# First attention layer of a two-block network: TensorE takes the next step's scores at the end of a step instead of at its start

## The chip, the cores and the metric

The kernel runs on one core of one Trainium2 chip. The metric is the device time of one execution in microseconds, as the median over several executions. A lower number is better. In the text TensorE is PE (its weight loads PEld), VectorE is DVE, ScalarE is ACT, GpSimd is POOL and SyncE is SP, as in the profile.

## What is computed

512 tokens of width 1024 go through two blocks. The first block is a recurrent and convolutional mixer and a layer that gathers expert rows for each token. The second has two attention layers, each followed by a SwiGLU layer. The change lies in the first of these attention layers only. For each head it adds three attentions over the same queries:

```python
s = einsum('bsgrd,bngd->bgrsn', q, k_cmp) * scale        # 31 compressed keys
p, denom, _ = masked_softmax(s + bias_c, dist_c >= 0)
o_cmp = einsum('bgrsn,bngd->bsgrd', p / maximum(denom, 1e-30), v_cmp)
...
o_sel = ...   # selected blocks of 64 keys; with 8 of 8 blocks all causal keys
o_win, _ = banded_attention(q, kwn, vwn, WIN - 1, 1, rel_bias)   # 256 keys back
o = g[..., 0:1] * o_cmp + g[..., 1:2] * o_sel + g[..., 2:3] * o_win
return o.reshape(B, S, D_MODEL) @ w_out
```

There are 16 heads of 64 channels and 4 groups of keys and values.

## The kernel before, in words

The program is written engine by engine, and each engine's queue is in the order of the Python code. Semaphores order the engines among each other. Nothing is scheduled automatically. The first attention layer's loop has 32 steps (STEPS = 8 * TT): eight pairs of heads, and for each pair four blocks of 128 queries (qt = s mod 4). A step handles the two heads of its pair, "half" 0 and 1, which sit on partitions 0 to 63 and 64 to 127. For each half there are three branches: "sel" with 128 (qt + 1) keys, "win" with at most 384, and "cmp" with 31. For one step, these are the pieces of work:

- `scores(s)` on PE (L1542): six products into four banks of the accumulator memory. "sel" has a bank of its own for each half, "win" and "cmp" share one. There is one set of banks, so a product waits until DVE has read that bank's scores of the step before (`bank_read`).
- `row_max(s)` on DVE (L1614): six instructions, each adding the bias table to the scores, writing the sum to `pA` and taking the row's extreme. It waits for `scores_ready`; its first instruction needs the first product, its second needs the fifth (`SCORES_BEFORE`).
- `exponentials(s)` on ACT (L1669), with the row sums.
- `inverse(s)` (L1632, L1634) and `scale(s)` (L1641, L1645) on DVE: the inverse of the row sums times the gates, then the scaling of all three branches of half 0 and the "sel" branch of half 1. POOL scales "win" and "cmp" of half 1 (L1704).
- `turn(s)` on PE (L1556): 6, 10, 14 or 16 transposes of the scaled weights, in chunks of four, into three banks in turn. A chunk with only half 0 needs `scaled`; one with half 1 needs POOL's `scaled_rest` too. A chunk also waits until the chunk three before has been copied out.
- `copies(s)` on ACT (L1592) and, for a step's last chunk, `last_copy(s)` on DVE (L1592 for full blocks, L1595 for the "cmp" blocks) into `ptA`.
- `values(s)` on PE (L1572): products of the transposed weights with the values, added up in one bank for both halves. It waits for all of the step's chunks in `ptA`.

The steps overlap. In iteration s, DVE does row_max(s), last_copy(s-2), inverse(s-1), scale(s-1); ACT does exponentials(s), copies(s-1). [...] SP loads the bias tables for a later pair of heads, released by `bank_read`.

Of the kernel before, what the change touches and what calls it, by code (L numbers as in the profile page):

```python
# [163 lines left out]
def program(nc, t):  # L164

    with ExitStack() as ctx:
# [1294 lines left out]
        STEPS = 8 * TT  # L1461
# [16 lines left out]
        def branches(s, half):  # L1478

            it, qt = divmod(s, TT)  # L1480
            gp = it // GR
            g, lo = 2 * gp + half, 64 * half
            rows, keys, cols = slice(lo, lo + 64), P * (qt + 1), slice(P * qt, P * qt + P)
            kv = slice(64 * g, 64 * g + 64)
            k0 = max(0, qt - 2)
            wide = keys - P * k0
            q, base = proj[rows, it, cols], 928 * half
            return {
                "sel": Branch(half, 2 * half, 0, keys, base, q, proj[rows, 12 + gp, 0:keys],
                              tabA[:, it % 2, half, 512 - keys:512], 1, [vtok[:, 0, x, kv] for x in range(qt + 1)]),  # L1490
                "win": Branch(half, 2 * half + 1, 0, wide, base + 512, q, proj[rows, 16 + gp, P * k0:keys],
                              tabA[:, it % 2, half, 896 - wide:896], 2, [vtok[:, 1, x, kv] for x in range(k0, qt + 1)]),
                "cmp": Branch(half, 2 * half + 1, 384, NCMP, base + 896, q, kcmp[rows, gp, :],
                              tcmp[:, heads(it)[half], 24 - 8 * qt:24 - 8 * qt + NCMP], 0, [vcmp[0:NCMP, kv]])}
# [6 lines left out]
        def turn_list(s):  # L1501

            sides = [branches(s, half) for half in range(2)]
            full = [(half, b) for half in range(2) for x in ("sel", "win") for b in sides[half][x].blocks]
            return full + [(half, sides[half]["cmp"].blocks[0]) for half in range(2)], len(full)

        def turn_chunks(s):

            order, full = turn_list(s)
            whole = full // 4 * 4  # L1510
            return [order[x:x + 4] for x in range(0, whole, 4)] + [order[whole:]]

        def chunk_no(s):

            return sum(len(turn_chunks(x)) for x in range(s))
# [5 lines left out]
        def chunk_copied(eng, s, c):  # L1521

            if c == len(turn_chunks(s)) - 1:
                eng.wait_ge(LA.last_copied, s + 1)
            else:
                eng.wait_ge(LA.pt_copied, act_chunks(s) + c + 1)
# [4 lines left out]
        def turn_bank(no):  # L1531
            return TURN_BANKS[no % len(TURN_BANKS)]

        def nsa_pe(pe, compressed_values):
            bank_of = {}

            def scores(s):
                for x, (name, half) in enumerate(PE_ORDER):
                    b = branches(s, half)[name]
                    if s:  # L1540
                        pe.wait_ge(LA.bank_read, PER * (s - 1) + READS_BEFORE[x])
                    pe.matmul(b.scores, b.q, b.keys, start=True, stop=True).then_inc(LA.scores_ready, 1)  # L1542

            def turn(s):
                for c, chunk in enumerate(turn_chunks(s)):
                    no = chunk_no(s) + c
                    turns = len(TURN_BANKS)
                    if no - turns in bank_of:
                        chunk_copied(pe, *bank_of[no - turns])
                    bank_of[no] = s, c  # L1550
                    other = max(half for half, _ in chunk)
                    pe.wait_ge(LA.scaled, 2 * s + 1 + other)
                    if other:
                        pe.wait_ge(LA.scaled_rest, s + 1)
                    for x, (_, (at, width, _)) in enumerate(chunk):
                        tr = pe.transpose(ps[0:width, turn_bank(no), P * x:P * x + P], pA[:, s % 3, at:at + width], ident)  # L1556
                    tr.then_inc(LA.turned, 1)

            def values(s):
                it, qt = divmod(s, TT)  # L1560
                for c in range(len(turn_chunks(s))):
                    chunk_copied(pe, s, c)
                if s == 0:
                    pe.wait_ge(cmp_copied, 2)
                if qt == 0 and it:
                    pe.wait_ge(LA.o_drained, it)
                order, _ = turn_list(s)
                sides = [[(x, b) for x, (half, b) in enumerate(order) if half == side] for side in range(2)]
                for y in range(len(sides[0])):
                    for half in range(2):  # L1570
                        x, (_, width, v) = sides[half][y]
                        mm = pe.matmul(ps[64 * half:64 * half + 64, OUT_BANK, P * qt:P * qt + P], v,  # L1572
                                       ptA[0:width, s % 2, P * x:P * x + P], start=y == 0, stop=y == len(sides[0]) - 1)
                mm.then_inc(LA.pv_done, 1)

            scores(0)
            compressed_values()
            for s in range(STEPS + 2):
                if s + 1 < STEPS:
                    scores(s + 1)  # L1580
                if s >= 2:
                    values(s - 2)
                if 1 <= s <= STEPS:
                    turn(s - 1)

        def copy_chunk(copy, s, c, done):

            chunk = turn_chunks(s)[c]
            full = sum(width == P for _, (_, width, _) in chunk)
            src, dst = bank(turn_bank(chunk_no(s) + c)), ptA[:, s % 2, 512 * c:512 * c + P * len(chunk)]  # L1590
            if full:
                ins = copy(dst[:, 0:P * full], src[:, 0:P * full])  # L1592
            if full < len(chunk):
                w = chunk[-1][1][1]
                ins = copy(dst[0:w, P * full:P * len(chunk)], src[0:w, P * full:P * len(chunk)])  # L1595
            ins.then_inc(done, 1)
# [426 lines left out]
        def layer_a_pe(pe):  # L2023
# [57 lines left out]
            pe.wait_ge(vt_copied, 4)  # L2081
            pe.wait_ge(cmp_copied, 1)
            nsa_pe(pe, compressed_values)
            pe.wait_ge(LA.o_drained, 8)
            out_project(pe, "a_out", "a_o")
# [985 lines left out]
```

## Time and profile before

| | before |
|---|---|
| median of 3 runs | 2892.04 us (2891.43 to 2892.5) |
| profiled execution | 2893.09 us, span 2891.0 us |
| PE busy | 2705.6 us (94%) |
| DVE busy | 1883.0 us (65%) |
| POOL busy | 1185.4 us (41%) |
| ACT busy | 843.4 us (29%) |
| the loop of the change, 1603.40 to 1757.90 | 154.50 us; PE 146.78, PEld 112.79, DVE 130.69, ACT 130.00, POOL 53.10 busy |

The profile comes from one profiled execution. The span is the time between the first and the last instruction; the rest of the execution's time lies around it. A busy share is an average over all stages, and the loop in question is 5% of the span. PE's matmuls overlap in the array, so their busy time is not time at its peak. "Granted clock" is TensorE's clock as a share of 2.4 GHz.

### The profile page before, as it was taken

How to read it: one execution, taken by the hardware profiler on the slowest of the kernel's cores; microseconds unless marked ns; L12 is line 12 of the kernel's file. 1: busy time of each engine (PE TensorE's matmuls, PEld its weight loads, DVE VectorE, ACT ScalarE, POOL GpSimd, SP SyncE). 2: the span in 40 equal slices, each digit the busy share in tenths (PEclk: the TensorE clock that was granted, in tenths of full speed). 3: DMA queues.
4: the chain of work that ended last, by engine and by line, in shares of the span. 5: the costliest groups of instructions: out<-in, count | busy, mean ns of one | idle time of the engine just before them, and what ended most of it. 6: DMA issues, size and time to landing. Idle time of an engine off the chain costs nothing.

```text
span 2891.0 us, 35803 instructions
## 1 busy us (share of the span) xinstructions
PE 2705.6 (94%) x12080; PEld 1729.4 (60%) x12080; DVE 1883.0 (65%) x4890; ACT 843.4 (29%) x1653; POOL 1185.4 (41%) x837
## 2 busy tenths in 40 slices
PE   8999999999877777799999999999999999999999
PEld 3364454444333332344447777888888877788887
DVE  8997888888888888778766786444223336554411
ACT  4731211111111111121123785222132127522222
POOL 5314444444444444444440233444444434444443
PEclk9999999999999999999999999999999999999999
DMA  4169999999999999999996121222323222222322
GB/s 132 61 236 371 418 414 418 421 421 420 417 421 419 420 421 414 419 418 420 420 420 239 59 69 59 95 94 94 107 89 100 90 67 67 66 95 96 103 101 79
DMA packets 130308, 700.38 MB, mean 242 GB/s; under 512 B 16694, under 2 KB 28886, under 8 KB 64343
## 3 DMA queue, kind: packets, MB, share of 16 engines
q0 software_dynamic: 74352, 543.04, 45.6%
q1 hardware_dynamic: 54760, 153.30, 16.0%
q10 hardware_dynamic: 1072, 2.41, 0.2%
q8 instruction: 75, 1.23, 0.2%
q14 instruction: 49, 0.40, 0.0%
HBM read 696.41 MB, written 2.28 MB: 242 GB/s over the span
## 4 chain that ended last, share of the span: by engine, by line
PE 49%; DMA 18%; issue 14%; DVE 8%; POOL 7%; ACT 3%; POOLq 0%; DVEq 0%; SPq 0%; ACTq 0%
DMA arena<-in_peer_uv,arena 18%; PE ps L543 16%; PE ps L883 15%; POOL w_lo L420 6%; PE ps L2379 3%; DVE arena L1216 2%; PE ps L911 2%; ACT arena L1669 1%; PE ps L2031 1%; PE ps L795 1%; DVE arena L1227 1%; PE ps L1572 1%; PE ps L1556 1%; PE ps L773 1%; PE ps L1542 1%
## 5 line engine op out<-in xcount | busy, mean ns | idle before, releaser
L883 PE MATMUL ps<-arena 128*128 128x512 f32 x2048 | 955.9, 611 | 143.4 <-DVE arena L1227 142.9
L1350 POOL DMA_INDIRECT arena<-in_peer_uv,arena x512 | 570.2, 1114 | 783.2 <-PE ps L883 719.7
L883 PEld LDWEIGHTS ps<-arena 128*128 128x128 f32 x2048 | 383.6, 194 | 651.4 <-issue 384.5
L1216 DVE CUSTOM_DVE_ANT_0 arena<-arena,sq 128x1024 f32<-128x1024 f32 x512 | 607.3, 1224 | 192.5 <-DMA arena<-in_peer_uv,arena 189.5
L420 POOL TENSOR_TENSOR w_lo<-ring,w_hi 128x1024 fp32r<-128x1024 f32 (+1 forms) x156 | 407.3, 2611 | 514.9 <-ACT w_hi L433 514.9
L543 PE MATMUL ps<-n_hi,w_hi 128*128 128x512 f32 x992 | 388.0, 391 | 0.5 <-issue 0.3
L543 PE MATMUL ps<-n_hi,w_lo 128*128 128x512 f32 x992 | 386.5, 390 | 0.0
L543 PE MATMUL ps<-n_lo,w_hi 128*128 128x512 f32 x992 | 382.4, 390 | 0.2 <-DVE n_lo L470 0.2
L1043 ACT ACTIVATE dots_gel<-dots_gel,tok_scale 128x2 f32<-128x2 f32 x256 | 75.7, 296 | 1000.0 <-DVE dots_gel L1216 999.7
L433 ACT CAST w_hi<-ring 128x1024 fp32r<-128x1024 f32 (+1 forms) x156 | 174.6, 1119 | 644.4 <-PE ps L543 644.4
L543 PEld LDWEIGHTS ps<-n_hi,w_hi 128*128 128x128 f32 x992 | 186.3, 188 | 40.5 <-issue 2.4
L543 PEld LDWEIGHTS ps<-n_lo,w_hi 128*128 128x128 f32 x992 | 186.3, 188 | 40.0 <-DVE n_lo L470 0.8
L543 PEld LDWEIGHTS ps<-n_hi,w_lo 128*128 128x128 f32 x992 | 186.3, 188 | 38.7
L1227 DVE TENSOR_SCALAR arena<-consts,dots_gel,tcmp 128x128 f32<-128x128 f32 x512 | 161.6, 368 | 30.5 <-ACT dots_gel L1043 15.5
L599 DVE TENSOR_TENSOR h<-ps,h 128x512 f32<-128x512 f32 x32 | 22.1, 691 | 218.9 <-PE ps L543 218.9
L1425 DVE TENSOR_TENSOR arena<-ps,rstd 128x512 f32<-128x512 f32 x44 | 30.4, 692 | 200.4 <-PE ps L543 200.4
L543 PE MATMUL ps<-hid_hi,w_hi 128*128 128x512 f32 x352 | 137.3, 390 | 1.3 <-POOL w_lo L420 1.3
L543 PE MATMUL ps<-hid_lo,w_hi 128*128 128x512 f32 x352 | 137.1, 390 | 0.0
L543 PE MATMUL ps<-hid_hi,w_lo 128*128 128x512 f32 x352 | 137.1, 390 | 0.0
L1704 POOL TENSOR_SCALAR arena<-arena 128x384 f32<-128x384 f32 (+2 forms) x64 | 53.1, 839 | 167.7 <-DVE arena L1634 167.7
L2379 PE MATMUL ps<-n,ring 128*128 128x512 f32 x256 | 114.0, 603 | 8.0 <-DMA ring<-in_w_in 7.8
L911 PE MATMUL ps<-n,ring 128*128 128x384 f32 x320 | 111.9, 487 | 0.0
(364 smaller groups left out, 3614.4 us busy)
## 6 DMA issues: line engine op xcount, KB each, us to landing
ring<-in_a_up SPq DMA_DIRECT2D x44, 512.0 KB, 3.5
ring<-in_b_up SPq DMA_DIRECT2D x44, 512.0 KB, 3.5
ring<-in_a_in SPq DMA_DIRECT2D x40, 512.0 KB, 7.8
ring<-in_b_q SPq DMA_DIRECT2D x24, 512.0 KB, 3.5
ring<-in_a_down SPq DMA_DIRECT2D x16, 704.0 KB, 4.1
ring<-in_b_down SPq DMA_DIRECT2D x16, 704.0 KB, 4.0
ring<-in_w_in SPq DMA_DIRECT2D x16, 512.0 KB, 3.5
arena<-in_peer_uv,arena POOLq DMA_INDIRECT x512, 10.8
```

The lines of the kernel that those rows point to most:

```text
L420: pool.tensor_tensor(w_lo[:, j % 2, 0:kt * P], ring[:, j, 0:kt * P], w_hi[:, j % 2, 0:kt * P], ALU.subtract).then_inc(split_lo, 1)
L433: act.copy(w_hi[:, j % 2, 0:kt * P], ring[:, j, 0:kt * P]).then_inc(split_hi, 1)
L543: mm = pe.matmul(bank(j // 2 if two else j), w[:, j % 2, cols], r[:, x, :], start=no == 0 and not (two and j % 2), stop=no == len(passes) ...
L883: mm = pe.matmul(bank(2 * (tt % 2) + q), diag[:, no % DIAGS, r, :], uvrow[p][r][:, D + 512 * q:D + 512 * q + 512], start=slot + r == 0, st ...
L911: mm = pe.matmul(ps[:, p % 2, 0:EARLY], ring[:, p % RING, k * P:(k + 1) * P], n[:, k, 0:EARLY], start=k == 0, stop=k == DK - 1)
L1043: act.activation(gel[:, p, :], dots[:, p, :], ACT.Gelu_apprx_tanh, scale=tok_scale[:, tt:tt + 1]).then_inc(gel_ready, 1)
L1216: ins = dve.tensor_tensor_reduce(out=u, in0=u, in1=ntok[:, tt, :], scale=1.0, scalar=0.0, op0=ALU.mult, op1=ALU.add, accum_out=dots[:, p, ...
L1227: ins = dve.tensor_scalar(diag[:, no % DIAGS, r, :], ident, gel[:, p, r:r + 1], gate_now[:, slot + r:slot + r + 1], ALU.mult, ALU.mult)
L1350: pool.indirect_dma_start(uvrow[p][r], None, t["peer_uv"], bass.IndirectOffsetOnAxis(ap=expert_id[:, tt, slot + r:slot + r + 1], axis=0)). ...
L1425: dve.tensor_tensor(gated[:, pr, :], bank(2 * pr + 1), rstd[:, :], ALU.mult).then_inc(tile_drained, 1)
L1704: ins = pool.tensor_scalar(pr, pr, invA[:, s % 3, 1, b.slot:b.slot + 1], None, ALU.mult)
L2379: mm = pe.matmul(bank(u % RING), ring[:, u % RING, k * P:(k + 1) * P], ns[k], start=k == 0, stop=k == DK - 1)
```

## The change

In `nsa_pe`, the iteration s of PE's loop issued scores(s+1), values(s-2), turn(s-1). Now it issues values(s-2), turn(s-1), scores(s+1). Nothing else is edited.

```diff
             for s in range(STEPS + 2):
-                if s + 1 < STEPS:
-                    scores(s + 1)
                 if s >= 2:
                     values(s - 2)
                 if 1 <= s <= STEPS:
                     turn(s - 1)
+                if s + 1 < STEPS:
+                    scores(s + 1)
```

The queue of PE in the middle of the loop, around the scores with 256 keys (L1542 scores, L1572 values, L1556 transposes), before:

```order
L1572 MATMUL ps<-arena 64x128 x10
L1556 MATMUL ps<-consts,arena 128x128 x12
L1556 MATMUL ps<-consts,arena 31x128 x2
L1542 MATMUL ps<-arena 128x256 x4
L1542 MATMUL ps<-arena 128x31 x2
L1572 MATMUL ps<-arena 64x128 x14
L1556 MATMUL ps<-consts,arena 128x128 x14
L1556 MATMUL ps<-consts,arena 31x128 x2
L1542 MATMUL ps<-arena 128x384 x4
```

The same place with the change:

```order
L1572 MATMUL ps<-arena 64x128 x14
L1556 MATMUL ps<-consts,arena 128x128 x14
L1556 MATMUL ps<-consts,arena 31x128 x2
L1542 MATMUL ps<-arena 128x256 x4
L1542 MATMUL ps<-arena 128x31 x2
L1572 MATMUL ps<-arena 64x128 x16
L1556 MATMUL ps<-consts,arena 128x128 x4
L1556 MATMUL ps<-consts,arena 31x128 x2
L1542 MATMUL ps<-arena 128x384 x4
```

The scores with 256 keys stood ahead of 14 products with the values and 16 transposes, and now stand behind them. The cyclic order scores, values, transposes is the same; what changes is which step's scores stand between a step's transposes and the next values: those of one step earlier.

The start of the loop, as the difference of PE's queue with its waits left out:

```order
 L1542 MATMUL ps<-arena 128x256 x4
 L1542 MATMUL ps<-arena 128x31 x2
+L1556 MATMUL ps<-consts,arena 128x128 x4
+L1556 MATMUL ps<-consts,arena 31x128 x2
 L1542 MATMUL ps<-arena 128x384 x4
 L1542 MATMUL ps<-arena 128x31 x2
-L1556 MATMUL ps<-consts,arena 128x128 x4
+L1572 MATMUL ps<-arena 64x128 x6
```

The scores of steps 0 and 1 keep their place; from step 2 on (128x384) a step's scores come behind the transposes of the step two before. The queues of DVE, ACT, POOL and SP are the same in both kernels.

## Rows read from the trace of the kernel before

**Rows 1.** Busy time by stretch: one round of four steps of the loop

```profile
core 0: us, PE busy (x) PEld busy (x) DVE busy (x) ACT busy (x) POOL busy (x), PEclk, DMA share, GB/s
1655.39:1673.95 18.56, 18.04 (x187) 13.89 (x188) 16.27 (x84) 15.97 (x59) 6.64 (x9) 1.00 0.17 57
```

**Rows 2.** Waits in the whole loop, 1603.4 to 1758 us

```profile
engine line waited for: us in total, times, longest us
...
DVE arena L1595 <- PE ps L1556: 10.8, 15, 2.1
...
DVE arena L1592 <- PE ps L1556: 7.1, 8, 2.0
...
PEld ps L1542 <- DVE arena L1614: 4.1, 18, 0.7
```

**Rows 3.** Timeline of one round, TensorE: start, duration, instruction, [idle before]

```profile
start us, us, engine line op out<-in xcount [idle before <-releaser]
...
1657.42 1.27 PE L1542 MATMUL ps<-arena 64*128 64x256 f32 x12
...
1660.46 2.04 PE L1556 MATMUL ps<-consts,arena 128*128 128x128 f32 x16
...
1662.44 1.70 PE L1542 MATMUL ps<-arena 64*128 64x384 f32 x12
...
1664.07 2.12 PE L1572 MATMUL ps<-arena 128*64 128x128 f32 x32
...
1666.12 0.87 PE L1556 MATMUL ps<-consts,arena 128*128 128x128 f32 x6
...
1666.93 1.92 PE L1542 MATMUL ps<-arena 64*128 64x512 f32 x12
```

**Rows 4.** Timeline of the same round, VectorE and GpSimd

```profile
1657.53 0.41 DVE L1595 COPY arena<-ps 31x256 f32<-31x256 f32 x1 [1.01 <-PE ps L1556]
...
1658.34 2.08 POOL L1704 TENSOR_SCALAR arena<-arena 128x384 f32<-128x384 f32 x2 [2.69 <-DVE arena L1634]
...
1660.49 0.42 DVE L1614 CUSTOM_DVE_ANT_0 arena<-ps,arena 128x256 f32<-128x256 f32 x1
...
1661.74 0.08 DVE L1614 DVE_READ_ACCUMULATOR2_ANT arena<- 128x1 f32 x1
...
1662.55 0.43 DVE L1592 COPY arena<-ps 128x256 f32<-128x256 f32 x1 [0.72 <-PE ps L1556]
...
1662.89 0.40 DVE L1595 COPY arena<-ps 31x256 f32<-31x256 f32 x1
...
1665.02 0.55 DVE L1614 CUSTOM_DVE_ANT_0 arena<-ps,arena 128x384 f32<-128x384 f32 x1
...
1666.67 0.08 DVE L1614 DVE_READ_ACCUMULATOR2_ANT arena<- 128x1 f32 x1
...
1667.84 1.49 POOL L1704 TENSOR_SCALAR arena<-arena 128x256 f32<-128x256 f32 x2 [3.03 <-DVE arena L1634]
...
1669.68 0.55 DVE L1614 CUSTOM_DVE_ANT_0 arena<-ps,arena 128x384 f32<-128x384 f32 x1
...
1671.46 0.41 DVE L1595 COPY arena<-ps 31x256 f32<-31x256 f32 x1
...
1672.26 1.94 POOL L1704 TENSOR_SCALAR arena<-arena 128x384 f32<-128x384 f32 x2 [2.93 <-DVE arena L1634]
```

**Rows 5.** Timeline, second iteration: GpSimd's scaling and the transposes it releases

```profile
1608.76 1.12 POOL L1704 TENSOR_SCALAR arena<-arena 128x128 f32<-128x128 f32 x2 [76.38 <-DVE arena L1634]
...
1609.99 0.61 PEld L1556 LDWEIGHTS ps<-consts,arena 128*128 128x128 f32 x6 [0.75 <-DVE arena L1645]
```

**Rows 6.** Timeline of the first two steps, where VectorE waits for scores

```profile
1603.43 0.86 PE L1542 MATMUL ps<-arena 64*128 64x128 f32 x12
...
1604.32 0.29 DVE L1614 CUSTOM_DVE_ANT_0 arena<-ps,arena 128x128 f32<-128x128 f32 x1
...
1605.18 0.08 DVE L1614 DVE_READ_ACCUMULATOR2_ANT arena<- 128x1 f32 x1
...
1605.41 1.52 PEld L1542 LDWEIGHTS ps<-arena 64*128 64x128 f32 x14
...
1606.72 0.42 DVE L1614 CUSTOM_DVE_ANT_0 arena<-ps,arena 128x256 f32<-128x256 f32 x1
```

**Rows 7.** Busy time by stretch: 1000 us of the expert stage

```profile
300.00:1300.00 1000.00, 869.53 (x2226) 392.25 (x2225) 834.43 (x2436) 162.33 (x341) 436.19 (x398) 0.98 1.01 419
```

## The prediction

> **What bounds the stage now.** I read the views in this order: busy time by stretch, the waits of the stage, then the timeline of one round of four steps. The edited loop is the compressed/selected/window attention of the first attention layer: 32 steps, in rounds of four that repeat. Step s has 1 to 4 key blocks (s mod 4 = 0 to 3); I call these widths 1 to 4. One round takes 18.56 us, and TensorE shows 18.04 us of it busy, VectorE 16.27, ScalarE 15.97, at a granted clock of 1.00 [rows 1]. So three engines are nearly full at once, which works only because each has something of another step to do while it waits. Over the whole loop VectorE idles 10.8 + 7.1 us for the transposes of a step's last chunk, and TensorE idles 4.1 us for VectorE's reading of the scores [rows 2]. Those are the only waits that this order of TensorE's work could be charged with; together 22 us.
>
> TensorE's busy time taken by itself would say that TensorE is the bound, and that its own order of work is then worth nothing: no change. The Trainium skill, Perfetto Trace Analysis, section Identifying the Most-Contended Engine, says that matmul busy time is no good measure and that the weight loads' share is better. By that reading there is slack here, since the loads are busy 13.89 of 18.56 us [rows 1]; the argument below needs only the order of dependences.
>
> In the timeline of the round [rows 3, 4], TensorE does scores, values, transposes, and again scores. VectorE reduces the scores of step s+1 while TensorE does values and transposes of older steps; at 1660.49 a reduction is under way and at 1660.46 the transposes start. The scores it reads (block at 1657.42) had been made 2.7 us before. That distance is the cover that the change takes away.
>
> **The change.** Nothing is added or removed: TensorE issues the same instructions, there is no DMA among them, and the other engines' queues are unchanged. 30 blocks of scores (steps 2 to 31) move from ahead of values(s-2) and turn(s-1) to behind them. turn(s-1) waits for scale(s-1) of VectorE and for the part that GpSimd scales. So the scores of s+1 now wait, through the queue, for scale(s-1); and VectorE's next work after scale(s-1) is the row reductions of s+1. Before, VectorE went from scale(s-1) into the reductions without a stop. Now it stands still while TensorE finishes the transposes and makes the scores. Values and transposes cannot slip earlier to pay for it, because values(s-2) need VectorE's last copy of s-2, which it issues behind the reductions of step s.
>
> The new cycle per step has three terms: VectorE's last copy, T from the end of that copy to the end of the transposes, and U from there to the end of the next row reductions.
>
> *Last copy.* 0.41 us where only two small blocks are copied (three of four steps), and 1662.55 to 1662.89 plus 0.40 = 0.74 us where there are two copies [rows 4]. Sum of a round 3 x 0.41 + 0.74 = 1.97 us. Its former waits of 1.01 and 0.72 us in these rows go, because the transposes are long done by then; that gain is inside this sum.
>
> *T.* GpSimd starts its scaling 0.40 us after the last copy ends (1657.53 + 0.41, then 1658.34) and takes 2.08, 1.49 and 1.94 us for the transposed steps of width 4, 2 and 3 [rows 4]. The first four transposes need only VectorE's half and come before it ends; the others wait for GpSimd. 16 transposes take 1660.46 to 1662.44 = 1.98 us and six 1666.12 to 1666.93 = 0.81 us [rows 3], so about 0.11 us each and 0.2 us to the next block. From GpSimd's last write to TensorE's next weight load is 0.11 us (1608.76 + 1.12, then 1609.99) [rows 5]. Hence, with the transposes behind the first four:
> width 4: 0.40 + 2.08 + 0.11 + 12 x 0.11 + 0.2 = 4.11;
> width 2: 0.40 + 1.49 + 0.11 + 6 x 0.11 + 0.2 = 2.86;
> width 3: 0.40 + 1.94 + 0.11 + 10 x 0.11 + 0.2 = 3.75.
> For width 1 the longer way is through the values of a width 4 step, 1664.07 to 1666.12 = 2.05 us [rows 3], so 0.11 + 2.05 + 0.81 = 2.97. Sum 13.69 us.
>
> *U.* The second reduction of a step needs five of the six score products, since window and compressed scores share a bank. The trace has two cases where VectorE stands waiting, as it will now always: the first two steps [rows 6]. At width 1 the second reduction starts 1604.32 - 1603.43 = 0.89 us after the block of scores, whose own busy time is 0.86; at width 2 it starts 1606.72 - 1605.41 = 1.31 us after, beside a block of 1.27 in the round [rows 3]. So it is the block plus 0.04. Blocks of width 3 and 4 take 1.70 and 1.92 us [rows 3], which gives 1.74 and 1.96. From the second reduction to the last: 1604.32 to 1605.18 = 0.86 [rows 6], 1660.49 to 1661.74 = 1.25, 1665.02 to 1666.67 = 1.65, 1669.68 to 1671.46 = 1.78 [rows 4]. U is 1.75, 2.56, 3.39, 3.74; sum 11.44 us.
>
> **Sum.** 1.97 + 13.69 + 11.44 = 27.10 us a round in place of 18.56 [rows 1]: +8.54, or 2.13 us a step. Times 30 moved blocks: **+64 us**. ScalarE's exponentials and copies (15.97 us busy per round) and GpSimd (6.64) fit in 27.1 us and stay off this cycle. Nothing later hides it: the products behind the loop need the last head's output. The profiled execution took 2893.1 us, 2.1 outside its span; it lies 1.1 above the median 2892.04. 2892 + 64 = **2956 us**.
>
> Bounds. Low: U supposes that a wide block must be nearly finished before the second reduction. If at every width it started after 0.89 us, as at width 1 [rows 6], a round would save 0.42 + 0.85 + 1.07 = 2.34, over 7.5 rounds 18 us: 2938. I take the block's length because width 2 follows it. High: each step gains two hand-overs that I price at 0.11 and 0.04. Were each 0.3 longer, a little above the mean idle of weight loads on VectorE in the loop (4.1 us over 18 times is 0.23) [rows 2], 30 x 0.6 = 18 us come on top: 2974.
>
> **Rivals.**
> - *TensorE's clock falls.* Its 18.04 busy us a round [rows 1] will stand in 27.1 us, 67% instead of 97%. In the expert stage, where TensorE shows 869.53 of 1000 us busy with waits between, the granted clock averages 0.98 [rows 7]: short falls from 2.4 to 1.2 GHz. At that rate it costs a few us here. If it stayed at 1.2 GHz throughout, the parts of TensorE on the cycle (transposes 1.52 + 0.81 + 0.86 + 1.30, values 2.05, scores 0.86 + 1.27 + 1.70 + 1.92 = 12.3 us a round) would double: +92 more, 3048. Against it: the idle gap of a step is at most 3.74 - 1.92 + 0.41 + 0.11 = 2.3 us (width 4), and rows 1 show 1.00 with many transposes. Full drop 4%, a partial one (above 2980) 6%.
>  The Trainium skill, TensorE: Matmul & The Clock Gate, Part 4: PE-mode transpose, says transposes do not count as busy work for the clock gate. By that rule the fall is likelier than I make it, with the same 3048 at the worst; the trace before, at 1.00 with transposes a third of TensorE's work, does not bear it out, though scores and values stood beside them.
> - *Faster.* If the reduced scores were not needed as soon as I say, the 10.8 + 7.1 + 4.1 us of rows 2 would vanish and nothing come in: 2870. It decides where transposes and scores end before VectorE is through with scale(s-1). The transposes wait for that very scaling, so this needs the dependence to be other than written: 2%.
> - *No change.* TensorE is really the bound and keeps its 18.04 us a round back to back, the order being immaterial: 2892. Busy shares speak for it, the chain through scale(s-1) against it: 3%.
> - *Half of it.* Faster VectorE and ScalarE instructions without contention, or a T where most transposes end before GpSimd does. Taking 0.7 us off each step's 2.13 leaves 43 us (2935), taking 1.4 leaves 22 (2914): about 2925, 5%. For it: the durations of rows 3 and 4 come from a loop with all engines busy. Against it: no row there shows one of these dependences skipped.
>
> **Numbers.** The forecast (2938 to 2974) has 80%, and the rivals have 10, 2, 3 and 5%. The range is 2930 to 2982: it holds the forecast's bounds, the upper end of the half case and a mild loss of clock. What a measurement can tell from no change is about 0.2% (6 us): faster 2%, within 0.2% 3%, slower 95%.
>
> **What would show it.** The loop should last about 64 us longer. A round should take near 27 us. VectorE's row reductions (L1614) should wait on L1542 in nearly all of 30 steps, some 2 to 3 us each; its waits of L1595 and L1592 on L1556, 17.9 us, should be nearly gone. TensorE's weight loads should wait for L1595, and its transposes for L1641, L1645 or L1704. The mean duration of instructions should stay. The prediction is wrong if L1614 does not wait, if a round stays under 24 us, or if the granted clock in the loop is well below 1.00.

## The result and the profile after

The changed kernel takes 2998.78 us (median of 4 runs, 2992.16 to 2999.77) against 2891.73 before: ratio 1.0369, 95% interval 1.0357 to 1.0381. It is 107 us slower. Forecast were 64 us and 2956, with 2982 as the upper end; the direction was right, the size was not.

The page of the changed kernel, busy times and the slices of TensorE, VectorE and clock:

```profile
span 2997.6 us, 35803 instructions
...
PE 2747.9 (92%) x12080; PEld 1758.6 (59%) x12080; DVE 1885.0 (63%) x4890; ACT 850.7 (28%) x1653; POOL 1183.5 (39%) x837
...
PEclk9999999999999999999998787999999999999999
```

The number of instructions is the same. The one new thing is the dip of the clock line in the slices of the loop: 8, 7, 8, 7. Everything that was lost was lost there. From the first scores to the first product behind the loop it was 1603.43 to 1758.66, 155.2 us; it is 1602.04 to 1865.57, 263.5 us. That is 108.3 us more, and what comes before and after differs by under 2 us.

The loop as one stretch of the changed kernel:

```profile
core 0: us, PE busy (x) PEld busy (x) DVE busy (x) ACT busy (x) POOL busy (x), PEclk, DMA share, GB/s
1602.50:1866.00 263.50, 190.68 (x1503) 144.17 (x1500) 134.25 (x648) 137.84 (x470) 53.17 (x64) 0.80 0.10 30
```

TensorE shows 190.68 us of it busy (72%) where it had 97% of a round [rows 1]. For the same instructions that is yet more busy time than the 146.78 us of before, and the granted clock averages 0.80. To read the counts: in these traces a matrix product leaves two records of TensorE and a transpose one. So x28 of L1572 is 14 products, and x16 of L1556 is 16 transposes.

Waits of the changed kernel, 1603 to 1880 us (engine, line, whom for, total, times, longest):

```profile
DVE arena L1614 <- PE ps L1542: 115.8, 45, 4.8
...
ACT arena L1669 <- DVE arena L1614: 64.7, 30, 4.2
...
PE ps L1572 <- DVE arena L1595: 45.9, 24, 2.4
...
DVE arena L1595 <- PE ps L1556: 3.9, 1, 3.9
...
DVE arena L1592 <- PE ps L1556: 1.9, 1, 1.9
```

The row reductions (L1614) wait 115.8 us for the scores. In the kernel before, 1603.4 to 1758 us, that wait came twice, and not in the steady loop:

```profile
DVE arena L1614 <- PE ps L1542: 8.6, 2, 7.9
```

The old waits for the transposes, 10.8 and 7.1 us [rows 2], are down to one each at the loop's end. TensorE in turn waits for VectorE's last copy ahead of the values. Each of the two stands while the other works.

The most useful view is busy time by stretch, with a stretch for each step, from the end of one step's row reductions to the end of the next. The number behind PEld, DVE, ACT and POOL is the granted clock. Widths 4, 1, 2, 3, 4, 1, 2 of the changed kernel:

```profile
1745.30:1752.31 7.01, 4.16 (x34) 2.76 (x34) 4.52 (x21) 4.32 (x15) 1.49 (x2) 1.00 0.00 0
1752.31:1758.21 5.90, 4.02 (x46) 3.24 (x46) 3.65 (x21) 4.22 (x15) 1.95 (x2) 1.00 0.52 156
1758.21:1765.25 7.04, 5.13 (x56) 4.26 (x56) 4.33 (x23) 4.10 (x18) 2.08 (x2) 1.00 0.02 3
1765.25:1773.88 8.63, 6.06 (x50) 4.76 (x50) 4.23 (x24) 4.02 (x15) 1.13 (x2) 0.80 0.00 0
1773.88:1782.53 8.65, 5.78 (x34) 3.81 (x34) 4.53 (x23) 4.42 (x15) 1.49 (x2) 0.80 0.01 2
1782.53:1791.00 8.47, 7.02 (x46) 5.86 (x46) 3.65 (x23) 4.42 (x15) 1.95 (x2) 0.60 0.88 261
1791.00:1798.03 7.03, 5.13 (x56) 4.26 (x56) 4.31 (x21) 4.09 (x18) 2.08 (x2) 1.00 0.29 117
```

At a clock of 1.00, widths 4, 1 and 2 take 7.01, 5.90 and 7.04 us. The prediction's terms give 7.01, 5.91 and 7.08. Widths 4 and 1 take 8.65 and 8.47 us where the clock was 0.80 and 0.60. So this one trace already separates the two parts of the loss, the new dependence and the clock, for three of the four widths. Of the 30 moved steps only nine ran at 1.00 throughout: the seven of width 2 and the one each of width 4 and width 1 shown here. No step of width 3 did.

The single instructions show both. Timeline of TensorE and VectorE in the changed kernel (start, duration):

```profile
1690.07 3.25 PE L1556 MATMUL ps<-consts,arena 128*128 128x128 f32 x14
...
1697.96 2.02 PE L1556 MATMUL ps<-consts,arena 128*128 128x128 f32 x16
...
1699.91 1.27 PE L1542 MATMUL ps<-arena 64*128 64x256 f32 x12
1700.64 0.43 DVE L1614 CUSTOM_DVE_ANT_0 arena<-ps,arena 128x256 f32<-128x256 f32 x1 [2.51 <-PE ps L1542]
...
1701.21 0.42 DVE L1614 CUSTOM_DVE_ANT_0 arena<-ps,arena 128x256 f32<-128x256 f32 x1
...
1707.65 3.20 PE L1542 MATMUL ps<-arena 64*128 64x384 f32 x12
```

VectorE stood 2.51 us for the block of scores that begins at 1699.91, and its second reduction starts 1.30 us after the block's start (1.31 was taken, from [rows 6]). 14 transposes took 3.25 us in a slow stretch, 16 took 2.02 in a fast one; the scores of width 3 took 3.20 us instead of 1.70 [rows 3].

### The profile page after: what moved, and what is told of

Its sections match the earlier page's. It is cut to its first block, busy times and chain, and to the rows that moved or that the text cites. A ratio compares the mean times of both kernels' runs of the same rounds, so it can differ in the third digit from the quotient of the medians.

```text
span 2997.6 us, 35803 instructions
## 1 busy us (share of the span) xinstructions
PE 2747.9 (92%) x12080; PEld 1758.6 (59%) x12080; DVE 1885.0 (63%) x4890; ACT 850.7 (28%) x1653; POOL 1183.5 (39%) x837
## 4 chain that ended last, share of the span: by engine, by line
PE 51%; DMA 18%; issue 14%; DVE 10%; POOL 6%; ACT 1%; POOLq 0%; DVEq 0%; SPq 0%; ACTq 0%
DMA arena<-in_peer_uv,arena 17%; PE ps L543 16%; PE ps L883 14%; POOL w_lo L420 6%; PE ps L2379 3%; DVE arena L1216 2%; PE ps L1556 2%; PE ps L911 2%; PE ps L1542 2%; PE ps L1572 2%; DVE arena L1614 1%; PE ps L2031 1%; DVE arena L1227 1%; PE ps L795 1%; PE ps L773 1%
## 5 line engine op out<-in xcount | busy, mean ns | idle before, releaser
L1614 DVE CUSTOM_DVE_ANT_0 arena<-ps,arena 128x384 f32<-128x384 f32 (+3 forms) x128 | 58.1, 473 | 125.7 <-PE ps L1542 123.8
L1572 PE MATMUL ps<-arena 128*64 128x128 f32 (+1 forms) x736 | 66.6, 330 | 63.5 <-DVE arena L1595 45.9
```

The costliest lines, as they stand in the source:

```text
L1614: dve.tensor_tensor_reduce(out=pA[:, s % 3, b.at:b.at + b.width], in0=b.scores, in1=b.tab, scale=1.0, scalar=-FLOOR, op0=ALU.add, op1=ALU.min,
```

## The experiments

Theory A: of the 107 us, 64 are the dependence at full clock, and 43 are TensorE working at 1.2 GHz in about 0.4 of the loop. Theory B: the 43 us are other new waits, and the clock is a side effect of no weight. All runs are compared with the kernel before on the same chip.

**Filler products.** They give TensorE more to do where it idles.

```diff
+            def fill(s, ns):
+                it, qt = divmod(s, TT)
+                if qt == 0 and it:
+                    pe.wait_ge(LA.o_drained, it)
+                for _ in range(ns[(s + 2) % TT]):
+                    pe.matmul(ps[:, OUT_BANK, P * qt:P * qt + P], ident, ident, start=True, stop=True)
...
                 if s + 1 < STEPS:
                     scores(s + 1)
+                    if s >= 2:
+                        fill(s - 1, (5, 8, 8, 8))
```

> The changed order, plus products that nobody reads (identity times identity, 128 columns, into the part of the values' bank that the next values overwrite), issued behind each block of scores from step 3 on: 5 behind a width 1 block, 8 behind the others, 211 in all. They lie where TensorE idles for VectorE's reductions and last copy. Theory A (of the 107 us, 64 are the new dependence at full clock and 43 are TensorE's clock falling to 1.2 GHz in 0.4 of the loop): the granted clock in the loop returns to 0.97 or more, and the time falls to 2950 to 2970 although TensorE has more to do. Theory B (the 43 us are longer waits that have nothing to do with the clock, and the clock figure is a side effect): no gain, 2995 to 3015, since the added products lengthen TensorE's queue.

Measured: 2958.77 us (2956.71 to 2960.94), ratio to before 1.0233 (1.0216 to 1.0250). With 211 more products the kernel is 40 us faster than the changed one. Busy time by stretch, one round, widths 4, 1, 2, 3:

```profile
1697.99:1705.00 7.01, 6.26 (x53) 4.72 (x51) 4.52 (x21) 4.31 (x15) 1.49 (x2) 1.00 0.01 4
1705.00:1710.90 5.90, 5.07 (x56) 4.20 (x55) 3.65 (x23) 4.23 (x15) 1.94 (x2) 1.00 0.51 157
1710.90:1717.93 7.03, 6.83 (x72) 5.85 (x72) 4.32 (x21) 4.09 (x18) 2.08 (x2) 1.00 0.01 2
1717.93:1725.06 7.13, 6.94 (x72) 5.68 (x71) 4.22 (x22) 4.02 (x15) 1.13 (x2) 1.00 0.00 0
sum 27.07, PE 25.10 PEld 20.45 DVE 16.71 ACT 16.65 POOL 6.65; mean PE 6.28 PEld 5.11 DVE 4.18 ACT 4.16 POOL 1.66
```

A round takes 27.07 us; 27.10 was predicted. Theory B falls: with the clock at 1.00 the widths 4, 1 and 2 take what they took at 1.00 without filler (7.01, 5.90 and 7.04 us), so nothing but the clock came back. Left are 2958.8 against 2892, 67 us. A few of these are still clock, in the first two moved steps. They are the first two lines here; the third is the first of these steps in the run with half the filler, where the clock happened to stay:

```profile
1606.35:1614.73 8.38, 4.64 (x18) 2.92 (x18) 3.84 (x21) 4.52 (x19) 1.12 (x2) 0.55 0.00 0
1614.73:1623.77 9.04, 8.53 (x50) 6.22 (x50) 4.54 (x23) 4.37 (x15) 1.50 (x2) 0.66 0.01 2
1605.35:1611.57 6.22, 2.48 (x18) 1.68 (x18) 3.84 (x21) 4.41 (x19) 1.12 (x2) 1.00 0.01 3
```

From these rows the split of the loss can be estimated. The 30 moved steps last 137.7 us before and 244.3 us with the change. With the first at 6.22 us and the others at their full-clock times (7.01, 5.90, 7.03, 7.13) they would last 202.7 us. That makes 65 us of dependence and 42 us of clock.

**Filler transposes.** As above with `pe.transpose(...)` in place of `pe.matmul(...)`.

> As the run with filler products, but the fillers are transposes of the identity, same number, places and sizes. If transposes hold the clock as products do: the same time as with filler products, 2950 to 2970, granted clock 0.97 or more. If transposes do not count for the clock: granted clock in the loop near 0.80 as with the change and 2990 to 3010. The second is what the Trainium skill says, TensorE: Matmul & The Clock Gate, Part 4: PE-mode transpose.

Measured: 2963.24 us (2960.73 to 2964.83), ratio 1.0251 (1.0234 to 1.0268). From 1620 to 1830 us:

```profile
1620.00:1830.00 210.00, 167.49 (x1638) 128.88 (x1635) 126.92 (x597) 127.71 (x432) 53.63 (x62) 0.99 0.12 38
```

The granted clock is 0.99 where the changed kernel has 0.81 over the same stretch. The fillers are equal in number but not in work, as the two counts from 1602 to 1880 us show, first for products, then for transposes:

```profile
L1581 PE MATMUL ps<-consts 128*128 128x128 f32 x422 | 54.8, 282 | 0.0
L1581 PE MATMUL ps<-consts 128*128 128x128 f32 x211 | 29.4, 280 | 0.0
```

So the fair partner of this run is the half dose of products below (2960.44 us). Here transposes hold the clock about as products do. The Trainium skill (TensorE: Matmul & The Clock Gate, Part 4: PE-mode transpose) says that transpose mode does not count as busy in the same way and that the full clock does not engage for it. That is not borne out for the fp32 transposes of this loop; the one type that the section names is bf16. Each filler also loads its weights, and no run here has the one without the other.

**Half, a quarter, and an uneven half.** The same edit with `(2, 4, 4, 4)`, `(1, 2, 2, 2)` and `(0, 0, 7, 7)` products behind widths 1 to 4.

> As the run with filler products but with 2 (width 1) or 4 (others) products behind a block, about half of them. Theory A predicts a time between 2958.8 and 2998.8 that goes with the granted clock in the loop: about 2965 to 2985 at 0.85 to 0.95. Theory B (the fillers help by something else than the clock, as by keeping the queue full): the time falls with no matching change of the granted clock.

> As the run with half the fillers, halved again: 1 product behind a width 1 block, 2 behind the others, 7 a round. 14 a round held the granted clock at 1.00 just as 29 did. If the clock has a sharp limit somewhere below 14 a round, this one either also gives 2955 to 2962 at 1.00 or falls back to 2985 or more at about 0.85; if it goes gradually, it lies near 2975 at about 0.92.

> 14 products a round as in the run with half the fillers, but all behind two blocks: 7 each behind the scores of width 3 and width 4, none behind width 1 and 2. If the work in a whole round decides, the clock stays at 1.00 and the time at 2955 to 2962. If each stretch of a round decides for itself, it falls in the stretches around width 1, and the time is 2970 or more.

Measured: 2960.44 us (ratio 1.0245, 1.0228 to 1.0262), 2963.09 (1.0253, 1.0236 to 1.0271) and 2963.62 (1.0256, 1.0238 to 1.0273). From 1620 to 1830 us, in this order:

```profile
1620.00:1830.00 210.00, 169.76 (x1630) 131.36 (x1631) 129.15 (x588) 128.25 (x432) 55.73 (x62) 1.00 0.12 38
```

```profile
1620.00:1830.00 210.00, 157.70 (x1534) 120.55 (x1534) 126.89 (x596) 126.93 (x431) 52.62 (x61) 0.99 0.12 38
```

```profile
1620.00:1830.00 210.00, 166.60 (x1632) 130.94 (x1632) 127.65 (x595) 128.60 (x434) 54.42 (x62) 0.99 0.12 38
```

I had expected the half dose at 2965 to 2985 and a clock of 0.85 to 0.95; that missed. The other two lie just above the 2955 to 2962 given for a clock that holds, and below the 2970 and 2975 given for a clock that falls in part. Seven products a round, 51 in all, bring back nearly as much as 29 a round. They add little to TensorE's work: a width 4 step shows 4.79 us busy with the quarter dose and 4.16 us without, both at a clock of 1.00. The recovery is not in proportion to the work added. The uneven half does as well as the even one, so between these two placements it does not matter much where the filler lies. The differences among the filler runs are up to 5 us, and their intervals overlap. In the quarter, the uneven and the transpose run one later step each still falls, to 0.75 or 0.80, and lasts 1.1 to 1.6 us longer. The profile of the half dose is of the fastest of its four executions (2956.09 to 2966.72 us).

**Only width 3, only width 1.** One block of scores in four moves; for width 1 the 2 in the edit is a 0.

```diff
+                late = s >= 1 and (s + 1) % TT == 2
+                if s + 1 < STEPS and not late:
+                    scores(s + 1)
                 if s >= 2:
                     values(s - 2)
                 if 1 <= s <= STEPS:
                     turn(s - 1)
-                if s + 1 < STEPS:
+                if s + 1 < STEPS and late:
                     scores(s + 1)
```

> Only the scores of width 3 (8 of the 30 blocks: steps 2, 6, ... 30) move behind values and transposes; the others stay ahead. Theory A (each moved block costs a term of its own, the terms add up): the width 3 step goes from 4.93 to 0.72 (the old wait for the transposes, which stays here) + 7.10 = 7.82 us, the next step loses its old wait of 0.29, so +2.6 us each, 8 times = +21: 2910 to 2916, with the clock at 1.00 because TensorE stays about 87% busy. Rival (the terms are equal, 64/30 = 2.13 each, plus the clock): 17 us at full clock, and above 2918 if the clock falls even with one late block in four.

> Only the scores of width 1 (7 blocks: steps 4, 8, ... 28) move. Theory A: the width 1 step goes from 3.54 to 5.90 us, and the next step loses its old wait of 1.01 for the transposes, which are now done before: +1.35 each, 7 times = +9.5: 2900 to 2904, clock 1.00. Rival (equal terms): 15 us, 2907 or more.

Measured: 2912.68 us (2911.72 to 2913.58), ratio 1.0073 (1.0056 to 1.0090), which is +20.6 with +21 predicted; and 2901.64 (2900.41 to 2904.31), ratio 1.0036 (1.0022 to 1.0050), +9.6 with +9.5 predicted. A round of the first, widths 3, 4, 1, 2:

```profile
1688.88:1696.83 7.95, 6.77 (x62) 4.40 (x61) 4.30 (x22) 5.55 (x20) 1.12 (x2) 1.00 0.01 2
1696.83:1701.26 4.43, 4.43 (x38) 3.17 (x34) 4.36 (x23) 3.56 (x13) 1.49 (x2) 1.00 0.00 0
1701.26:1704.80 3.54, 3.14 (x38) 2.68 (x37) 3.47 (x22) 3.32 (x13) 1.94 (x2) 1.00 0.63 197
1704.80:1709.73 4.93, 4.93 (x58) 4.17 (x56) 4.22 (x22) 3.86 (x17) 2.08 (x2) 1.00 0.14 50
```

7.82 was worked out for width 3 and 7.95 came; the step behind it falls from 4.80 to 4.43, its old wait gone. The agreement of the sum is in part luck. A width 2 step also falls, from 5.29 to 4.93, which I had not foreseen, so a round is 2.29 us longer (20.85 against 18.56) and not 2.6. The first moved step makes up for it, since its clock fell:

```profile
1605.10:1613.48 8.38, 6.33 (x23) 3.63 (x24) 3.84 (x21) 4.52 (x19) 1.12 (x2) 0.59 0.01 2
```

A round with the width 1 block late is 20.12 us, 1.56 longer. Equal shares of 2.13 a block would have given 17 and 15 us in all. Width 1 excludes them. For width 3 the steady round, 2.29, is too near to 2.13 to decide. The agreement for width 1 is closer in the sum than in its parts: the step took 6.26 us where I had 5.90. There the 14 transposes take 2.06 us to the next block instead of 1.74, because the last two wait for ScalarE's copy of the first chunk, as they did before; with every block late that copy is done in time. With TensorE about 92% busy (129.10 of 140 us in the first, 18.47 of a 20.12 us round in the second) the clock stays at 1.00 in both, apart from that one step of the first.

**In the middle.** values(s-2), scores(s+1), turn(s-1).

> Half of the move: values(s-2), scores(s+1), turn(s-1). The scores no longer stand behind the transposes, so they do not wait for scale(s-1), but still behind the values. Theory A (the dependence through the transposes is what costs): TensorE's chain per step is last copy, values, scores, transposes; a round 1.97 + 6.24 + 5.7 + 5.83 + 4 x 0.16 = 20.4 us in place of 18.56, so +14 us over 30 steps, 2900 to 2915, clock 1.00. Rival (standing behind the values, which wait for VectorE's last copy, is what costs): most of the 107 us stays, 2960 or more.

Measured: 2916.01 us (2915.83 to 2917.59), ratio 1.0085 (1.0068 to 1.0102): +24, a little above the range given (+8 to +23), and far below 107. The rival falls: standing behind the values costs 24 us, standing behind the transposes too costs the rest. Some 4 of the 24 us are clock, in two steps of width 4 that take 7.63 and 6.74 us at 0.55 and 0.75, where the others take 5.20. Waits of this kernel, 1600 to 1780 us:

```profile
PEld ps L1572 <- ACT arena L1592: 39.7, 31, 1.6
DVE arena L1614 <- PE ps L1542: 35.4, 33, 8.0
PE ps L1572 <- DVE arena L1595: 24.7, 22, 1.4
```

The first of these lines is what my sum lacked: values also wait for ScalarE's copy of the transposes that were just made. A round takes 21.97 us, 20.4 was given.

**Values last.** turn(s-1), scores(s+1), values(s-2).

> turn(s-1), scores(s+1), values(s-2): the scores still behind the transposes, but the values of 0.95 to 2.05 us lie in the time in which VectorE reduces. At full clock only the width 1 transposes gain (they no longer wait for 2.05 us of values: 0.9 us in 8 steps), so about 2892 + 57 = 2949. Theory A1 (the clock follows the share of a stretch in which TensorE works, wherever the idle time lies): it falls as with the change, granted clock about 0.80, 2980 to 2995. Theory A2 (it follows the gap between scores and values, which this order closes, moving the idle time ahead of the transposes): clock near 1.00, 2945 to 2955.

Measured: 2976.09 us (2972.30 to 2977.73), ratio 1.0290 (1.0273 to 1.0307). Steps of width 4, 1, 3 and another of width 3:

```profile
1646.10:1653.11 7.01, 4.45 (x38) 2.85 (x38) 4.52 (x21) 5.56 (x18) 1.49 (x2) 1.00 0.00 0
1653.11:1661.10 7.99, 5.54 (x36) 5.08 (x38) 3.65 (x23) 4.42 (x15) 1.95 (x2) 0.58 0.41 118
...
1668.12:1676.03 7.91, 6.06 (x52) 4.28 (x50) 4.23 (x24) 2.65 (x11) 1.12 (x2) 0.78 0.01 3
1697.41:1703.98 6.57, 4.72 (x56) 3.47 (x54) 4.23 (x24) 2.65 (x11) 1.12 (x2) 1.00 0.00 0
```

Width 3 at full clock takes 6.57 us instead of 7.13, since the transposes of width 1 no longer stand behind values (0.9 had been given). Neither A1 nor A2 holds: the granted clock over 1620 to 1830 us is 0.86, between them, though TensorE's busy share is as with the change (149.82 and 152.63 of 210 us). Closing one gap and opening another helped a part. What decides is left open.

**Scores first, transposes ahead of the values.** scores(s+1), turn(s-1), values(s-2), the order before with its last two parts exchanged.

> The order before with its last two parts exchanged: scores(s+1), turn(s-1), values(s-2). If the distance between scores and their reductions is what matters, this keeps it; the transposes come earlier, so VectorE's waits of 10.8 + 7.1 us for them go, and TensorE's own work of about 17.8 us a round becomes the limit in place of 18.56: 2884 to 2892, possibly a little faster than before. Rival: TensorE idles ahead of the transposes for scale(s-1) and cannot make it good, 2900 or more.

Measured: 2902.58 us (2901.94 to 2905.27), ratio 1.0041 (1.0027 to 1.0055): 10 us slower where 2884 to 2892 was expected, the rival's side. Its timeline:

```profile
1695.07 1.50 PE L1556 MATMUL ps<-consts,arena 128*128 128x128 f32 x12 [1.29 <-DVE arena L1641]
...
1697.28 0.41 PE L1556 MATMUL ps<-consts,arena 128*31 128x128 f32 x2 [0.71 <-ACT arena L1592]
```

TensorE waits 1.29 us for the scaling, in a place where the order before gave it values to do, and 0.71 us for ScalarE's copy of the first chunk, which stands behind exponentials. A round takes 19.65 us in place of 18.56. No order tried here beats the one before.

## Why the prediction was right or wrong

- **Direction and mechanism: right.** The scores now wait for scale(s-1) through the transposes, and VectorE for the scores. L1614 waits on L1542; the old waits are gone, and VectorE waits 2.51 us in a width 2 step as forecast.
- **Last copy, T, U and their sum: right.** The loss at full clock is 65 us by the estimate above, and 64 were forecast. 27.10 us a round were worked out. The four steps at full clock with filler take 7.01 + 5.90 + 7.03 + 7.13 = 27.07, and each of the four is within 0.05 of its terms (7.01, 5.91, 7.08, 7.10). The choice between the bounds of U, block length and not 0.89 us, was the right one. One reading of the rows was loose and carried nothing: the 2.7 us of cover are counted from the start of the block of scores (1657.42), which ends at 1658.69, so the distance from its end to the first reduction at 1660.15 is 1.5 us.
- **Additivity: right in the main, with luck.** The two runs with one block in four gave +20.6 and +9.6 us for +21 and +9.5, but the parts agree less well. A round grew by 2.29 and 1.56 us, where 2.6 and 1.35 were given.
- **The failed step is the clock.** The sum has no term for it. The prediction put it at "a few us here", by the 0.98 of the expert stage [rows 7], and left it to a rival with 10% in all, 6% for a partial fall. It measured 0.80 over the loop and about 42 us. The filler runs show that these us are the clock's: with 0.99 to 1.00 they give back 35 to 40. It is the rival's mechanism, at less than half of its full price of 92 us: the clock was low in about 0.4 of the loop, and steps of 7.01 and 5.90 us then took 8.65 and 8.47. The prediction's own sign of being wrong, a granted clock well below 1.00, is what came. The expert stage was a poor measure. TensorE is 87% busy there, and I had in hand that it would go from 97% to 67% here. Its products are also 128 rows deep and 512 columns wide, while here scores and values use half of the array's rows or columns. Which of the two makes the difference was not tested, and why the clock falls in this loop stays open.
- **"The idle gap of a step is at most 2.3 us" was about true and no protection.** Each round's gaps of TensorE ahead of the values are 1.44, 2.18, 2.20 and 2.38 us. One longer gap, 3.34 us, stands ahead of the first transposes. The clock fell all along the loop.
- **The rule of the Trainium skill** on transposes (TensorE: Matmul & The Clock Gate, Part 4: PE-mode transpose) would have made a fall likelier, and a fall came. But the run with filler transposes does not bear out the reason.
- **Faster, no change, half:** excluded by the waits and the steps above.

## What to carry to other kernels

When TensorE's queue puts a product behind one that waits for an engine, that engine's next work inherits the whole wait. Distance between a product and its reader is what the first place in a step buys, and its price can be summed from rows: for the changed order 64 us for some 65. The same way of summing gave 14 us for the order in the middle, where 24 came, because one wait was left out. When such a change makes TensorE idle part of every step, cost the stage at the lower clock as well, and read the steps of one trace by their granted clock: those at 1.00 give the dependence, the others the clock. A width that never ran at 1.00, as width 3 here, needs a run that holds the clock.

## What had not been expected of the hardware

More work made the kernel faster: 211 products that nobody reads took 40 us off, and 51 took about 35 off (2998.8 to 2963.1), with the granted clock over the stretch going from 0.81 to 0.99. In the changed kernel the steps of width 2, with 16 transposes and 14 value products in 7.03 us, always ran at 1.00, and each fall came in a step of another width. 211 transposes of the identity held the clock (0.99) about as well as 102 products of it (1.00), at nearly the same TensorE time.
